# Strassen's product in four feed forward stages, its block products beside the down product

## The chip, the cores and the metric

The kernel runs on one core of one Trainium2 chip. The time is device microseconds of one execution. Two levels of TensorE's clock occur in such profiles, 1.2 and 2.4 GHz; the profile prints the granted one in tenths of full speed. The engines are TensorE (PE, with its weight loads as PEld), VectorE (DVE), ScalarE (ACT), GpSimd (POOL) and SyncE (SP, which only issues DMAs here).

## The reference

Two transformer blocks on 256 tokens of width 1024, all in float32. Eight stages follow one another: 0 feed forward, 1 attention and convolution, 2 feed forward, 3 feed forward, 4 gated linear attention, 5 feed forward (with these the first block is done), 6 the mixer of the second block, 7 its feed forward. All five feed forward stages compute the same kind of thing:

```python
def swiglu(x, w_in, w_out):
    a, b = jnp.split(x @ w_in, 2, axis=-1)
    return (jax.nn.silu(a) * b) @ w_out

# the first block, per layer
f = swiglu(rms_norm(h, g[0]), ffn1_w_in[l], ffn1_w_out[l])
h = h + FFN_RES * rms_norm(f, g[1])
# the second block
ffn = jnp.dot(jax.nn.silu(jnp.dot(h2, w_ffn_gate)) * jnp.dot(h2, w_ffn_up), w_ffn_down)
```

Here x is 256 x 1024, a and b have 2816 columns each, and w_out is 2816 x 1024. Besides, the second block needs `mod = silu(c) @ w_ada + b_ada` (1024 x 6144), which the kernel computes little by little beside the stages 0 to 5.

## The kernel before

**Exact products from split operands.** Each float32 operand is split in a high part (rounded to the type that TensorE multiplies fast) and the rest: `xh`, `xl` for the tokens, `whi`, `wlo` for the weights, `gh`, `gl` for the hidden values. A product is then three matmuls: high by high, high by rest, rest by high. Tokens are the stationary side (128 x 128), weights move (128 x 512), so one k block of 128 rows for one half of the tokens (`tok` 0 or 1) is three matmuls into one PSUM bank of 512 columns.

**Units and subunits.** `plan` is the list of weight units in the order of use: a unit is up to four k blocks of 512 columns (1 MB) and is loaded by SyncE into one of three `raw` buffers (`load_unit`, L480). Each unit gives subunits of two k blocks. For every subunit ScalarE writes `whi` (`split_hi`, L508) and VectorE `wlo` (`split_lo`, L524) into a ring of seven buffers (`NSPL`), and TensorE then spends 12 matmuls on it (6 for each half of the tokens). `whi` of subunit j waits for TensorE's last matmul on subunit j-7, and a unit's load waits for `wlo` of the unit three loads before it. ScalarE and VectorE walk the same list some five subunits ahead of TensorE (`ahead`, `LOOK`), and between the splits stand their other tasks, in the order in which the code is written: nothing is reordered at run time.

**A feed forward stage** has 11 chunks of 256 hidden columns. A chunk takes 256 columns of a and 256 of b (two units, four subunits, 48 matmuls), one bank for each half of the tokens. ScalarE then takes the silu (`act_silu`), VectorE multiplies (`dve_gate`) into `hid`, TensorE transposes the hidden values of two chunks at a time (`pe_hid_two`, L1143), ScalarE and VectorE split them (`act_ghi`, `dve_glo`). After the chunks comes the down product (`pe_down`, L854): 22 subunits of `w_out` (264 matmuls) into four banks, column half n = 0 or 1 by token half. At its end ScalarE squares the result, VectorE multiplies by a gain row and adds it to `h`, and the next stage opens.

**Strassen's product** is used in stage 7 alone (`STRASSEN = (7,)`). Chunks 8 and 9 together are x (256 x 1024) by a 1024 x 1024 block, which splits into four 512 x 512 blocks and two token halves by two k halves. Seven block products p1 to p7 of two subunits and 12 matmuls each (`pe_product`, L778) replace the eight of the plain way. Their moving sides are built by memory transfers that add: GpSimd issues them (`pool_strassen`, L561). p1's block is loaded into the tile `rows` (which elsewhere holds two gain rows), p5 adds a block to it, p3's block is loaded into `work`, p6 is the sum of both, made by VectorE (`dve_t2`, L543), then p4 adds a block to `rows` and p7 one to `work`. Each waits until the block before it in its tile has been split. p2 is a plain unit in the `raw` ring. The token sums are made by VectorE (`dve_sx`) and split like the rest into `sxh`, `sxl`. The seven results are combined in four banks a, b, c, d: ScalarE copies a at p1 (`act_part`, L819), and twice again, for VectorE's subtractions (`dve_combine`, L830), on which p3 and p4 wait. In stage 7 each product stands between two chunks (`sequence`): 0, 1, p1, 2, p2, 3, p5, 4, p6, 5, p3, 6, p7, 7, p4, 10.

**Beside it** SyncE's queue brings the 96 tiles of `w_ada` (256 KB each, `load_ada`, L637), one behind each of certain units; VectorE adds each into `adaacc` (L618), and twelve times folds a sum (`ada_sum`, L621). Each tile's load waits until VectorE has used the tile two before it, and SyncE issues nothing past that wait.

## Time and profile before

| | us |
|---|---|
| median of 3 runs | 1418.01 |
| lowest, highest | 1417.10, 1418.36 |
| the profiled execution, its own time | 1416.94 |
| its span in the profile | 1415.1 |
| TensorE busy | 1401.8 (99%) |
| VectorE busy | 956.5 (68%) |
| ScalarE busy | 731.7 (52%) |

Times in the profile run from the start of the span. Matmuls are pipelined, so that the time of one (389 ns in most rows) is longer than the distance from one to the next; a busy TensorE says that it is fed and not how fast it runs. An engine's idle time is put down to what released it. "Landing" is the time from a DMA's issue to its last byte.

### The profile page before, as it was taken

What the parts mean: (1) busy time and instruction counts of PE and PEld (TensorE: products, weight loads), DVE (VectorE), ACT (ScalarE), POOL (GpSimd) and SP (SyncE); (2) the same over time, 40 slices, a digit from 0 to 9 for tenths busy, and PEclk for the clock granted to TensorE, in tenths of its full rate; (3) what the DMA queues carried; (4) which work ended last, traced back from release to release, by engine and by line L of the source; (5) the groups of instructions that cost most, each with busy time, mean ns of one, the idle gap of its engine ahead of it and who ended that gap; (6) DMA issues with size and microseconds to landing.
All of it is one profiled execution on the core that took longest, in us unless ns stands there. A gap on an engine that the chain in (4) does not pass through costs nothing.

```text
span 1415.1 us, 19090 instructions
## 1 busy us (share of the span) xinstructions
PE 1401.8 (99%) x7327; PEld 1147.2 (81%) x7327; DVE 956.5 (68%) x1307; ACT 731.7 (52%) x1050; POOL 160.1 (11%) x242
## 2 busy tenths in 40 slices
PE   9999999999999999999999999999999999999997
PEld 7888888688888888888878888888877788888886
DVE  6666567886676667665787757755568566786654
ACT  6444455564443445543665545445655634655542
POOL 1600010000000000000172100000542110011000
PEclk9999999999999999999999999999999999999999
DMA  9585755256876778868544688764845355588551
GB/s 318 199 253 198 262 203 207 68 171 207 251 242 215 231 228 265 252 210 264 187 150 148 203 210 256 255 211 140 238 160 197 121 178 179 171 242 211 178 209 59
DMA packets 234857, 288.24 MB, mean 204 GB/s; under 512 B 37076, under 2 KB 156672, under 8 KB 234768
## 3 DMA queue, kind: packets, MB, share of 16 engines
q1 hardware_dynamic: 232160, 281.48, 61.6%
q0 software_dynamic: 2208, 5.24, 1.8%
q8 instruction: 58, 0.95, 0.3%
q10 hardware_dynamic: 400, 0.31, 0.1%
q14 instruction: 31, 0.25, 0.1%
HBM read 282.80 MB, written 4.20 MB: 203 GB/s over the span
## 4 chain that ended last, share of the span: by engine, by line
PE 95%; DVE 2%; issue 1%; ACT 1%; POOL 0%; POOLq 0%; ACTq 0%; DVEq 0%
PE ps L706 29%; PE ps L709 28%; PE ps L707 28%; PE pst L974 1%; PE pst L1155 1%; DVE wlo L532 1%; PE pst L1468 1%; PE ps L813 0%; PE ps L812 0%; PE ps L811 0%; PE ps L1415 0%; ACT whi L521 0%; PE ps L679 0%; PE pst L1782 0%; PE pst L2355 0%
## 5 line engine op out<-in xcount | busy, mean ns | idle before, releaser
L532 DVE TENSOR_TENSOR wlo<-raw,whi 128x1024 fp32r<-128x1024 f32 (+2 forms) x468 | 558.2, 1224 | 257.7 <-ACT whi L521 255.9
L521 ACT ACTIVATE whi<-raw 128x1024 fp32r<-128x1024 f32 (+2 forms) x468 | 467.8, 1040 | 244.2 <-PE ps L709 97.4
L706 PE MATMUL ps<-whi,xh 128*128 128x512 f32 (+4 forms) x1406 | 551.5, 392 | 1.6 <-ACT xh L1013 0.6
L707 PE MATMUL ps<-wlo,xh 128*128 128x512 f32 (+4 forms) x1406 | 541.1, 385 | 0.0
L709 PE MATMUL ps<-whi,xl 128*128 128x512 f32 (+4 forms) x1406 | 532.7, 385 | 0.0
L706 PEld LDWEIGHTS ps<-whi,xh 128*128 128x128 f32 x1406 | 263.9, 188 | 60.6 <-issue 4.7
L709 PEld LDWEIGHTS ps<-whi,xl 128*128 128x128 f32 x1406 | 263.9, 188 | 53.6
L707 PEld LDWEIGHTS ps<-wlo,xh 128*128 128x128 f32 x1406 | 264.2, 188 | 49.8
L706 PE MATMUL ps<-whi,gh 128*128 128x512 f32 x440 | 172.0, 391 | 0.0
L707 PE MATMUL ps<-wlo,gh 128*128 128x512 f32 x440 | 171.2, 389 | 0.0
L709 PE MATMUL ps<-whi,gl 128*128 128x512 f32 x440 | 153.4, 389 | 0.0
L1094 ACT ACTIVATE hid<-ps,st 128x256 f32<-128x256 f32 x88 | 41.3, 473 | 151.0 <-PE ps L709 151.0
L914 POOL TENSOR_SCALAR st<-st 128x1 f32<-128x1 f32 x26 | 10.5, 405 | 903.1 <-ACT work L900 903.1
L1100 DVE SCALAR_TENSOR_TENSOR hid<-ps,st,hid 128x256 f32<-128x256 f32 x88 | 41.8, 482 | 87.8 <-ACT hid L1094 87.7
L709 PEld LDWEIGHTS ps<-whi,gl 128*128 128x128 f32 x440 | 82.6, 188 | 17.3
L706 PEld LDWEIGHTS ps<-whi,gh 128*128 128x128 f32 x440 | 82.6, 188 | 16.9
L707 PEld LDWEIGHTS ps<-wlo,gh 128*128 128x128 f32 x440 | 82.6, 188 | 16.8
L618 DVE SCALAR_TENSOR_TENSOR adaacc<-adat,scol,adaacc 128x512 f32<-128x512 f32 x84 | 62.7, 746 | 0.0
L1170 ACT ACTIVATE gh<-pst 128x1024 fp32r<-128x1024 f32 x25 | 25.5, 1020 | 20.9 <-PE pst L1155 20.7
L1179 DVE TENSOR_TENSOR gl<-pst,gh 128x1024 fp32r<-128x1024 f32 x25 | 30.5, 1221 | 8.1 <-ACT gh L1170 8.1
L900 ACT ACTIVATE work<-h 128x512 f32<-128x512 f32 x36 | 22.4, 627 | 20.3 <-DVE h L2249 18.9
L1613 DVE SCALAR_TENSOR_TENSOR Y<-cx,vcol,Y 128x256 f32<-128x256 f32 x79 | 32.4, 480 | 0.0
(306 smaller groups left out, 956.0 us busy)
## 6 DMA issues: line engine op xcount, KB each, us to landing
raw<-in_ffn_w_in_dram SPq DMA_DIRECT2D x174, 512.0 KB, 5.3
raw<-in_ffn_w_out_dram SPq DMA_DIRECT2D x40, 1024.0 KB, 5.5
raw<-in_w_in_dram SPq DMA_DIRECT2D x26, 1024.0 KB, 4.8
adat<-in_w_ada_dram SPq DMA_DIRECT2D x96, 256.0 KB, 2.8
raw<-in_hyb_w_in_dram SPq DMA_DIRECT2D x10, 1024.0 KB, 5.1
raw<-in_gla_w_in_dram SPq DMA_DIRECT2D x10, 1024.0 KB, 5.2
raw<-in_w_ffn_down_dram SPq DMA_DIRECT2D x10, 1024.0 KB, 5.0
raw<-in_w_ffn_gate_dram SPq DMA_DIRECT2D x18, 512.0 KB, 3.9
```

The costliest lines, as they stand in the source:

```text
L521: e.activation(split_of(whi, j), raw_of(j), ACT.Copy).then_inc(*whi_made.up(j))
L532: e.tensor_tensor(split_of(wlo, j), raw_of(j), split_of(whi, j).bitcast(F32), ALU.subtract).then_inc(*wlo_made.up(j))
L618: e.scalar_tensor_tensor(adaacc[:, :], adat[n % 2][:, :], sc, adaacc[:, :], ALU.mult, ALU.add).then_inc(*ada_added.up(c, k))
L706: e.matmul(ps[:, 0:n], a, whi_of(j, k), start=first and k == 0, stop=False)
L707: last = e.matmul(ps[:, 0:n], a, wlo_of(j, k), start=False, stop=False)
L709: last = e.matmul(ps[:, 0:n], b, whi_of(j, k), start=False, stop=final and k == subs[j][2] - 1)
L900: e.activation(spare[:, 0:src.shape[1]], src, ACT.Square, scale=scale, accum_out=col(2, "ss", key)[:, i:i + 1]).then_inc(*squares.up(key, i))
L1094: e.activation(hb[:, tok * 512 + 256:tok * 512 + 512], acc.of(st, JC[st, c], tok)[:, 0:256], ACT.Silu, scale=rstd(("h", st, tok)) if st < ...
L1100: e.scalar_tensor_tensor(hb[:, tok * 512:tok * 512 + 256], acc.of(st, JC[st, c], tok)[:, 256:512], rstd(("h", st, tok)) if st < 7 else 1.0 ...
L1170: e.activation(halves_of(gh[:, c * 512:(c + 2) * 512]), turned_halves, ACT.Copy).then_inc(*ghi_made.up(st, c))
L1179: e.tensor_tensor(halves_of(gl[:, x]), turned_halves, halves_of(gh[:, x]).bitcast(F32), ALU.subtract).then_inc(*glo_made.up(st, c))
L1613: e.scalar_tensor_tensor(y_of(b), cx_of(b, k), conv_w(b, k), y_of(b), ALU.mult, ALU.add).then_inc(*tap_made.up(b, k))
```

## The change

Stages 2, 3, 5 and 7 now take chunks 8 and 9 by Strassen's product. Their order is new, in stage 7 too: chunks 0 to 7, p1, chunk 10, and then the down product, in whose first columns the other six products stand. The down product of these stages goes through 16 k blocks for column half 0, through the same for half 1, and then through the last six for both (before: four k blocks for half 0, the same for half 1, and so on). With i the number of the down subunit, p5 stands ahead of i = 2, p6 ahead of 4, p3 and p2 ahead of 6, p7 ahead of 10, p4 ahead of 12 (`BESIDE`). The banks of column half 1 are the ones that b and d leave. The hidden values of chunks 8 and 9 are transposed at i = 14 and used from i = 16 on.

The token sums are spread over chunks 3 to 5. The tiles of `w_ada` skip the units that have no load on SyncE's queue, so they stand a little closer. The gain rows of these stages are loaded in the middle of the down product, since `rows` holds weight blocks until then. Two small transfers that write gate values to memory (4 KB, element by element) are now eight pieces each.

```diff
@@ -279,16 +279,18 @@
                         plan.append(([(w[k * P:(k + m) * P, n * 512:(n + 1) * 512]
                                        .rearrange("(k p) n -> p k n", p=P), 0, 512)], m, 512))
 
-        STRASSEN = (7,)
+        STRASSEN = (2, 3, 5, 7)
         PAIR = 8
         BLOCK = {"p1": ("x1", 0, 0), "p2": ("ring", 1, 0), "p5": ("x1", 0, 1), "p6": ("x1", None, None),
                  "p3": ("x2", 1, 1), "p7": ("x2", 0, 1), "p4": ("x1", 1, 0)}
-        product_unit, home, chunk_unit, down_unit = {}, {}, {}, {}
+        BESIDE = {2: ("p5",), 4: ("p6",), 6: ("p3", "p2"), 10: ("p7",), 12: ("p4",)}
+        mixed_units = [(k, min(4, k1 - k), n) for k0, k1 in ((0, 16), (16, 22)) for n in range(2) for k in range(k0, k1, 4)]
+        product_unit, home, chunk_unit, down_unit, down_units = {}, {}, {}, {}, {}
 
         def sequence(st):
 
             if st in STRASSEN:
-                return (0, 1, "p1", 2, "p2", 3, "p5", 4, "p6", 5, "p3", 6, "p7", 7, "p4", 10)
+                return (*range(8), "p1", 10)
             return tuple(range(11))
 
...
@@ -314,7 +316,15 @@
                 else:
                     plan_parts([(w, c * 256, 256) for w in w_in], 8)
             down_unit[st] = len(plan)
-            plan_down(w_out, 22)
+            if st not in STRASSEN:
+                plan_down(w_out, 22)
+                return
+            for i, (k, m, n) in enumerate(mixed_units):
+                for name in BESIDE.get(2 * i, ()):
+                    plan_product(st, w_in, name)
+                down_units.setdefault(st, []).append(len(plan))
+                plan.append(([(w_out[k * P:(k + m) * P, n * 512:(n + 1) * 512]
+                               .rearrange("(k p) n -> p k n", p=P), 0, 512)], m, 512))
 
 
         GLA_COLS = (((512, 512),), ((256, 256), (3072, 16)), ((0, 256),), ((1024, 512),), ((1536, 512),), ((2048, 512),),
...
@@ -400,14 +411,15 @@
 
 
         ada_view = T["w_ada_2"].rearrange("(p k) n -> p k n", k=8)
-        ada_units = [u for st in (0, 2, 3, 5) for u in range(U0[st] + (8 if st == 0 else 0), U0[st + 1])]
+        ada_units = [u for st in (0, 2, 3, 5) for u in range(U0[st] + (8 if st == 0 else 0), U0[st + 1]) if u not in home]
...
@@ -538,7 +550,7 @@
                     if u in ada_summed:
                         ada_sum(e, ada_summed[u])
 
...
@@ -564,10 +576,10 @@
                 e.wait_ge(*wlo_made.at(last_sub[product_unit[st, name]]))
             e.wait_ge(*f_scaled.at(st - 1, 1, 1))
             pool_product(e, st, "p1", False)
+            e.wait_ge(*xlo_made.at(st, "sums", 1))
+            pool_product(e, st, "p3", False)
             split("p1")
             pool_product(e, st, "p5", True)
-            e.wait_ge(*xlo_made.at(st, "sums"))
-            pool_product(e, st, "p3", False)
             split("p6")
             pool_product(e, st, "p4", True)
             split("p3")
...
@@ -778,19 +798,19 @@
         def pe_product(e, st, name, base):
 
             bank, tile, first, until = {
-                "p1": ("a", 4, True, (silu_made, st, PAIR, 1)), "p2": ("b", None, False, None),
-                "p5": ("c", 5, True, (gated, st, PAIR, 1)), "p3": ("d", 3, False, (gated, st, PAIR, 0)),
+                "p1": ("a", 0, True, (silu_made, st, PAIR, 1)), "p2": ("b", None, False, None),
...
             if name == "p1":
-                acc.next((st, "b"), (silu_made, st, PAIR, 0), tile=base + 2)
+                acc.next((st, "b"), (silu_made, st, PAIR, 0), tile=base + 3)
                 b_freed[st] = acc.freed
             ps = acc.of(st, bank)
             if name == "p5":
-                e.wait_ge(*xlo_made.at(st, "sums"))
+                e.wait_ge(*xlo_made.at(st, "sums", 1))
             if name == "p2":
                 e.wait_ge(*part_made.at(st, "p1"))
...
@@ -830,6 +850,8 @@
         def dve_combine(e, st, name):
 
             e.wait_ge(*part_made.at(st, name))
+            if name == "p6":
+                e.wait_ge(*gated.at(st, 10, 1))
             d = acc.of(st, "d" if name == "p6" else "c")
             e.tensor_tensor(d[:, :], acc.of(st, "c")[:, :], part[:, :], ALU.subtract
...
+        def down_sub(j0, i):
+            return DSUB[j0][i] if j0 in DSUB else j0 + i
+
+        def mixed_order():
+            return [(q, n) for k, m, n in mixed_units for q in range(k, k + m, 2)]
...
@@ -857,21 +885,28 @@
 
 
             bank, freed = {}, {}
-            for tok in range(2):
-                for n in range(2):
-                    bank[tok, n] = acc.next((key, tok, n), *readers(tok, n))
-                    freed[tok, n] = acc.freed
-            order = down_order(nk)
+
+            def take(tok, n, tile=None):
+                bank[tok, n] = acc.next((key, tok, n), *readers(tok, n), tile=tile)
+                freed[tok, n] = acc.freed
+            mixed = j0 in DSUB
+            if not mixed:
+                for tok in range(2):
+                    for n in range(2):
+                        take(tok, n)
+            order = mixed_order() if mixed else down_order(nk)
 
             def one(i, tok):
                 q, n = order[i]
                 if q == 0:
+                    if mixed:
+                        take(tok, n, acc.n + 2 + 2 * tok + n)
                     for done in freed[tok, n]:
                         e.wait_ge(*done)
...
@@ -1187,20 +1226,16 @@
                 enter(e, st, 0)
                 pe_warm(e, 4)
             pe_first(e, st, j0, lambda: enter(e, st, 1), readers)
-            base = acc.n - 4
             for c in sequence(st)[2:]:
                 if c in BLOCK:
-                    pe_product(e, st, c, base)
-                    if c == "p4":
-                        pe_hid_two(e, st, PAIR - 2)
+                    pe_product(e, st, c, acc.n)
                     continue
 
                 def at(i, c=c):
-                    if c % 2 == 0 and i == (3 if st in STRASSEN and c == 10 else 2):
-                        pe_hid_two(e, st, c - 2)
-                pe_chunk(e, st, JC[st, c], readers[c], at, (base, base + 1) if st in STRASSEN else (None, None))
-            if st in STRASSEN:
-                acc.n += 4
+                    if c % 2 == 0 and i == 2:
+                        pe_hid_two(e, st, before(st, c))
+                mixed = c == 10 and st in STRASSEN
+                pe_chunk(e, st, JC[st, c], readers[c], at, (acc.n + 1, acc.n + 5) if mixed else (None, None))
 
         def entry(e, st):
 
...
@@ -1213,6 +1248,11 @@
             j1 = JD[st]
 
             def at(i):
+                if st in STRASSEN:
+                    for name in BESIDE.get(i, ()):
+                        pe_product(e, st, name, acc.n)
+                    if i == 14:
+                        pe_hid_two(e, st, PAIR)
                 if i == 2:
...
@@ -1222,37 +1262,44 @@
                     lambda q, tok: (ghi_made.at(st, turn_of(q // 2)), glo_made.at(st, turn_of(q // 2))), readers, at, lag=LAG[st],
                     then=entry(e, st + 1))
 
...
-                    if st in STRASSEN and (c, i) == (2, 1):
-                        act_sx(e, st)
+                    if mixed and (c, i) == (10, 2):
+                        act_part(e, st, "p1")
+                    if mixed and (c, i) in SX_HI:
+                        act_sx(e, st, SX_HI.index((c, i)))
                 if c % 2 == 0:
-                    act_ghi(e, st, c - 2)
+                    act_ghi(e, st, before(st, c))
                 act_silu(e, st, c, 0)
                 act_silu(e, st, c, 1)
             for i in range(22):
-                act_begin(e, JD[st] + i)
+                for name in BESIDE.get(i, ()) if mixed else ():
+                    for half in range(2):
+                        act_begin(e, JP[st, name] + half)
+                act_begin(e, down_sub(JD[st], i))
                 if i == 2:
                     act_ghi(e, st, 10)
+                if mixed and i in (5, 11):
+                    act_part(e, st, "p6" if i == 5 else "p7")
+                if mixed and i in (7, 13):
+                    act_silu_pair(e, st, i // 13)
+                if mixed and i == 15:
+                    act_ghi(e, st, PAIR)
 
         def dve_ffn(e, st):
             j0 = J0[st]
...
@@ -2952,14 +3003,19 @@
             pool_diags(e)
             pool_open(e, 1)
             pool_open(e, 2)
+            pool_strassen(e, 2)
             pool_open(e, 3)
+            pool_strassen(e, 3)
             pool_gla(e)
             pool_open(e, 5)
+            pool_strassen(e, 5)
             pool_m2(e)
             pool_ada_open(e, 7)
             pool_strassen(e, 7)
             for tok in range(2):
                 pool_pow(e, ("h", 8, tok))
+
+        gate_piece = {u0 + b: (which, b) for which, u0 in ((2, U0[5] + 10), (5, U0[6] + 8)) for b in range(8)}
 
         def sp_program(e):
             for i, n in enumerate((0, 512)):
@@ -2984,17 +3040,19 @@
                         e.dma_start(wg[:, :], T["gla_w_gate"][0]).then_inc(*s_wg.up())
                     if st == 6:
                         load_row(e, "gn", T["gn_w_2"], D, [gla_normed.at(1, 3)])
-                if u in (U0[5] + 10, U0[6] + 8):
-                    i, which = (0, 2) if u < U0[6] else (1, 5)
-                    e.wait_ge(*mod_made.at(2 * which + 1))
-                    e.dma_start(gate_rows[i].rearrange("(b p) -> p b", p=P), modc[:, which * 8:which * 8 + 8],
-                                allow_slow_non_contiguous=True).then_inc(*s_gates.up(which))
-                if u == U0[6] + 10:
+                if u in gate_piece:
+                    which, b = gate_piece[u]
+                    if b == 0:
+                        e.wait_ge(*mod_made.at(2 * which + 1))
+                    e.dma_start(gate_rows[which // 5][b * P:(b + 1) * P].rearrange("(p o) -> p o", o=1),
+                                modc[:, which * 8 + b:which * 8 + b + 1], allow_slow_non_contiguous=True
+                                ).then_inc(*s_gates.up(which))
+                if u == U0[6] + 16:
                     load_row(e, "g2", gate_rows[0], D, [s_gates.at(2), f_scaled.at(5, 1, 1)])
-                if u == (down_unit[7] if 7 in STRASSEN else U0[7] + 4):
+                if u == (down_units[7][8] if 7 in STRASSEN else U0[7] + 4):
                     load_row(e, "g5", gate_rows[1], D, [s_gates.at(5), gr_made.at(1, 1), *rows_free(7)])
                 for st in STRASSEN:
-                    if u == down_unit[st] and st in gains:
+                    if u == down_units[st][8] and st in gains:
                         load_row(e, st, gains[st], D, rows_free(st))
                 if u == U0[4] + 7:
                     o = const_at["lev"][0]
```

Two places in the program's order, all in stage 2 (the others are alike). In the rows `whi` and `wlo` are the parts of a subunit of weights, and what they are made from tells what it is: `raw` a plain unit, `rows` p1, p5, p6 or p4, `work` p3 or p7.

VectorE before, from the gates of chunk 10 (L1100) into the down product:

```order
L1100 SCALAR_TENSOR_TENSOR hid<-ps,st,hid 128x256 x2
L532 TENSOR_TENSOR wlo<-raw,whi 128x1024 x3
L1175 TENSOR_TENSOR gl<-pst,gh 128x512
L532 TENSOR_TENSOR wlo<-raw,whi 128x1024
L615 TENSOR_SCALAR adaacc<-adat,scol 128x512
L532 TENSOR_TENSOR wlo<-raw,whi 128x1024 x2
L618 SCALAR_TENSOR_TENSOR adaacc<-adat,scol,adaacc 128x512
```

The same place now:

```order
L1136 SCALAR_TENSOR_TENSOR hid<-ps,st,hid 128x256 x2
L560 TENSOR_TENSOR rows<-rows,work 128x2048
L544 TENSOR_TENSOR wlo<-raw,whi 128x1024 x2
L544 TENSOR_TENSOR wlo<-rows,whi 128x1024 x2
L638 SCALAR_TENSOR_TENSOR adaacc<-adat,scol,adaacc 128x512
L544 TENSOR_TENSOR wlo<-raw,whi 128x1024
L1214 TENSOR_TENSOR gl<-pst,gh 128x512
L544 TENSOR_TENSOR wlo<-raw,whi 128x1024
L544 TENSOR_TENSOR wlo<-work,whi 128x1024 x2
L544 TENSOR_TENSOR wlo<-raw,whi 128x1024 x2
L856 TENSOR_TENSOR ps<-ps,part 128x512
```

Between the last gate of chunk 10 and the subtraction (L856) that p3 waits for stand the sum of p6 (L560), ten splits and two smaller operations.

ScalarE now, from the splits of p3 (`work`, the second row) to the silu of token half 0 of chunks 8 and 9 (L1153), which leaves bank b:

```order
L533 ACTIVATE whi<-raw 128x1024
L533 ACTIVATE whi<-work 128x1024 x2
L533 ACTIVATE whi<-raw 128x1024 x2
L847 ACTIVATE part<-ps 128x512
L533 ACTIVATE whi<-raw 128x1024 x4
L533 ACTIVATE whi<-work 128x1024 x2
L1153 ACTIVATE hid<-ps,st 128x2x256
```

ScalarE before, from chunk 10 on, had splits of plain units and nothing else in the down product (the last row):

```order
L521 ACTIVATE whi<-raw 128x1024 x4
L1170 ACTIVATE gh<-pst 128x2x8x64
L1094 ACTIVATE hid<-ps,st 128x256 x2
L521 ACTIVATE whi<-raw 128x1024 x3
L1168 ACTIVATE gh<-pst 128x512
L521 ACTIVATE whi<-raw 128x1024 x17
```

The copy (L847) and the silu now stand among the splits, and the silu stands behind the two splits of p7.

GpSimd, whose queue had nothing but the small operations of the norms in stages 2, 3 and 5, now issues ten half-unit transfers in each of them, ahead of the norms of the next stage: two for p1, two for p3, then two each that add, for p5, p4 and p7.

## Rows read from the trace of the kernel before

**Rows 1.** The page: engines, TensorE's clock over 40 slices, the chain by engine.
```profile
PE 1401.8 (99%) x7327; PEld 1147.2 (81%) x7327; DVE 956.5 (68%) x1307; ACT 731.7 (52%) x1050; POOL 160.1 (11%) x242
...
PEclk9999999999999999999999999999999999999999
...
PE 95%; DVE 2%; issue 1%; ACT 1%; POOL 0%; POOLq 0%; ACTq 0%; DVEq 0%
```

**Rows 2.** Chain of waits in order of time: start us, us, what.
```profile
336.81 0.64 PE pst L1155 x16
...
427.36 0.64 PE pst L1155 x16
...
821.22 0.64 PE pst L1155 x16
...
911.77 0.64 PE pst L1155 x16
...
1256.16 0.65 PE pst L1155 x16
...
1343.99 0.65 PE pst L1155 x16
```

**Rows 3.** Timeline of TensorE: start us, us, line, operation; first and last of 27.
```profile
299.63 0.39 PE L706 MATMUL ps<-whi,xh 128*128 128x512 f32 x1
...
305.53 0.39 PE L709 MATMUL ps<-whi,xl 128*128 128x512 f32 x1
```

**Rows 4.** Instruction groups, shapes apart, whole span: busy us, mean ns.
```profile
L618 DVE SCALAR_TENSOR_TENSOR adaacc<-adat,scol,adaacc 128x512 f32<-128x512 f32 x84 | 62.7, 746 | 0.0
...
L811 PE MATMUL ps<-whi,sxh 128*128 128x512 f32 x16 | 6.2, 389 | 0.0
```

**Rows 5.** The same for VectorE, window 1240 to 1350 (stage 7).
```profile
L532 DVE TENSOR_TENSOR wlo<-raw,whi 128x1024 fp32r<-128x1024 f32 x35 | 41.3, 1220 | 5.4 <-ACT whi L521 5.4
...
L548 DVE TENSOR_TENSOR rows<-rows,work 128x2048 f32<-128x2048 f32 x1 | 2.3, 2291 | 0.0
L605 DVE TENSOR_TENSOR sxl<-work,sxh 128x2048 fp32r<-128x2048 f32 x1 | 2.3, 2282 | 0.0
L834 DVE TENSOR_TENSOR ps<-ps,part 128x512 f32<-128x512 f32 x2 | 1.4, 693 | 0.0
...
L589 DVE TENSOR_TENSOR work<-xh,xl 128x1024 f32<-128x1024 f32 x1 | 1.2, 1215 | 0.0
```

**Rows 6.** The same for ScalarE, same window.
```profile
L521 ACT ACTIVATE whi<-raw 128x1024 fp32r<-128x1024 f32 x37 | 37.3, 1053 | 4.3 <-DMA raw<-in_w_ffn_up_dram 3.5 <-PE ps L709 0.8
...
L827 ACT ACTIVATE part<-ps 128x512 f32<-128x512 f32 x2 | 1.2, 580 | 0.0
```

**Rows 7.** Timeline of GpSimd's DMA issues, stage 7.
```profile
1266.36 1.50 POOL L559 DMA_DIRECT2D work<-in_w_ffn_up_dram  x2 [18.58 <-DVE sxl L605]
1282.43 2.48 POOL L557 DMA_DIRECT2D rows<-in_w_ffn_gate_dram  x2 [14.57 <-DVE wlo L532]
1296.89 2.42 POOL L557 DMA_DIRECT2D work<-in_w_ffn_up_dram  x2 [11.98 <-DVE wlo L532]
```

**Rows 8.** Timeline of ScalarE beside them.
```profile
1309.15 1.06 ACT L521 ACTIVATE whi<-work 128x1024 fp32r<-128x1024 f32 x1 [1.73 <-DMA work<-in_w_ffn_up_dram]
```

**Rows 9.** DMA queues, window 1278 to 1311: packets, MB, share of 16 engines.
```profile
q1 hardware_dynamic: 5371, 5.33, 52.0%
q0 software_dynamic: 1088, 2.10, 38.6%
```

**Rows 10.** Windows: length, busy us by engine, clock, DMA share, GB/s.
```profile
872.00:883.00 11.00, 11.00 (x50) 9.13 (x49) 6.95 (x9) 4.86 (x6) 0.00 (x0) 1.00 0.81 229
1289.00:1300.00 11.00, 11.00 (x50) 9.09 (x49) 8.36 (x9) 6.95 (x9) 2.42 (x2) 1.00 0.89 220
```

**Rows 11.** DMA issues, whole span: KB each, median us to landing.
```profile
raw<-in_ffn_w_out_dram SPq DMA_DIRECT2D x40, 1024.0 KB, 5.5
...
gate_rows<-modc SPq DMA_DIRECT2D x2, 4.0 KB, 12.4
```

More of the change, by code:

```diff
@@ L360, in program @@
         JD = {st: first_sub[u] for st, u in down_unit.items()}
+        DSUB = {JD[st]: [j for u in us for j in range(first_sub[u], last_sub[u] + 1)] for st, us in down_units.items()}
         JC = {key: first_sub[u] for key, u in chunk_unit.items()}
@@ new lines, in act_sx, with dve_sx_lo @@
+        def act_sx(e, st, half):
+            o = slice(half * 1024, (half + 1) * 1024)
+            e.wait_ge(*summed.at(st, "x", "p3"))
+            e.activation(sxh[:, o], workx[:, o], ACT.Copy).then_inc(*xhi_made.up(st, "sums", half))
+        def dve_sx_lo(e, st, half):
+            o = slice(half * 1024, (half + 1) * 1024)
+            e.wait_ge(*xhi_made.at(st, "sums", half))
+            e.tensor_tensor(sxl[:, o], workx[:, o], sxh[:, o].bitcast(F32), ALU.subtract
+                            ).then_inc(*xlo_made.up(st, "sums", half))
@@ L888, in down_last @@
         def down_last(j0, nk, n):
-            return j0 + max(i for i, (q, m) in enumerate(down_order(nk)) if m == n)
+            order = mixed_order() if j0 in DSUB else down_order(nk)
+            return down_sub(j0, max(i for i, (q, m) in enumerate(order) if m == n))
         halves = Ring([junk[:, 0:512], junk[:, 512:1024]])
@@ L1126, in dve_gate_pair, with before @@
                                    ).then_inc(*gated.up(st, PAIR, tok))
+        def before(st, c):
+            return 6 if c == 10 and st in STRASSEN else c - 2
         def turn_of(c):
@@ L1223, in pe_ffn, with act_ffn @@
                     then=entry(e, st + 1))
-        COMBINE = {2: "p1", 5: "p6", 7: "p7"}
-        def act_ffn(e, st, before):
+        SX_AT = [(3, 0), (3, 1), (3, 2), (3, 3), (4, 0)]
+        SX_HI, SX_LO = [(5, 0), (5, 2)], [(5, 1), (5, 3)]
+        def act_ffn(e, st, opening):
             j0 = J0[st]
@@ L1231, in act_ffn @@
             else:
-                act_open(e, st, before, lambda tok: act_silu(e, st, 0, tok))
+                act_open(e, st, opening, lambda tok: act_silu(e, st, 0, tok))
+            mixed = st in STRASSEN
             for c in sequence(st)[1:]:
@@ L1273, in dve_ffn @@
                     dve_begin(e, JC[st, c] + i)
[L1274 to L1275 removed]
+                    if mixed and (c, i) in SX_AT:
+                        dve_sx(e, st, SX_AT.index((c, i)))
+                    if mixed and (c, i) in SX_LO:
+                        dve_sx_lo(e, st, SX_LO.index((c, i)))
                 if c % 2 == 0:
[L1277 removed]
+                    dve_glo(e, st, before(st, c))
                 dve_gate(e, st, c, 0)
                 dve_gate(e, st, c, 1)
[L1280 to L1283 removed]
             for i in range(22):
[L1285 removed]
+                for name in BESIDE.get(i, ()) if mixed else ():
+                    for half in range(2):
+                        dve_begin(e, JP[st, name] + half)
+                dve_begin(e, down_sub(JD[st], i))
                 if i == 2:
                     dve_glo(e, st, 10)
+                if mixed and i in (5, 11):
+                    dve_combine(e, st, "p6" if i == 5 else "p7")
+                if mixed and i in (7, 13):
+                    dve_gate_pair(e, st, i // 13)
+                if mixed and i == 15:
+                    dve_glo(e, st, PAIR)
         hyb_gate = sig("hyb_gate")
```

79 lines of the change are left out of this document (32 added, 47 removed).

## The prediction

> **What bounds the kernel now.** The page comes first: TensorE is busy for 1401.8 of 1415.1 us, its clock shows full speed in all 40 slices (that is 2.4 GHz), and the chain that ends last is 95% TensorE [rows 1]. So time goes only where TensorE has fewer matmuls, or stands still less; VectorE at 68% and ScalarE at 52% have room on the average, and what is to be asked of them is whether they are late at one place.
>
> Next, what a matmul costs. From the first to the last of 27 matmuls in a row it takes 305.53 - 299.63 = 5.90 us for 26 distances, 0.227 us each [rows 3]; the 0.39 us printed for one is its length in the pipeline. A subunit or a block product (12 matmuls) is 2.72 us.
>
> Then, what Strassen's product has brought where it is already used. The chain shows the transposes of hidden chunks 0 and of chunks 8: between them lie 8 chunks, 384 matmuls, in the plain stages, and they take 427.36 - 336.81 = 90.55 us in stage 2 and 911.77 - 821.22 = 90.55 in stage 5. In stage 7, p1 lies ahead of the first and one subunit more ahead of the last, so there are 372, and they take 1343.99 - 1256.16 = 87.83 us [rows 2]. The difference is 2.72 us for 12 matmuls, just their own time: the block products of stage 7 cost TensorE no wait. A matmul on the token sums takes the same 389 ns as the others [rows 4].
>
> **The change part by part.**
>
> *Removed.* In each of stages 2, 3 and 5, eight blocks of 12 matmuls become seven. 3 x 12 x 0.2267 us = 8.16 us off TensorE. Stage 7 had seven already: nothing. Transposes are as many as before.
>
> *Added on VectorE*, per new stage, by the rows of stage 7 [rows 5]: 1.2 (sum of the parts of x), 4 x 0.7 (token sums, of the size of a combination), 2.3 (their rest, now in two halves), 2.3 (p6's sum), 2 x 0.69 (combinations), less two splits of 1.22 each since there are 14 subunits and not 16. That is 10.0 - 2.4 = 7.6 us in a stage of some 187 us, in which a plain stage leaves VectorE a third of its time. *On ScalarE*: 1.9 for the sums and 3 x 0.58 for copies, less 2 x 1.05 [rows 6]: 1.5 us. Both lie beside TensorE. On the average they cost nothing; so the places where TensorE waits for one of them are worked through.
>
> *p3 waits for the combination of c and p6's copy.* Behind p6 TensorE has two down subunits, 5.44 us. VectorE must have done, from the last gate of chunk 10 on: 2.3 + 10 x 1.22 + 0.75 + 0.7 = 16.0 us of other work, by the order shown ahead of L856 [rows 4, 5]. It starts some 1.4 us behind chunk 10's last matmul (a silu and a gate), so it is through at 17.4. TensorE reaches p6's end after two down subunits, p5, two more and p6: 4 x 2.72 + 2 x 2.72 = 16.3 us. Copy (0.58) and subtraction (0.69) then end near 18.7, and p3 starts at 21.8. There are 3 us to spare. For the first subunit behind p6's sum it is 1.4 + 2.3 + 1.22 = 4.9 against 8.2. p4's wait for the second combination has two subunits of cover as well, and less work ahead of it. The transposes of chunks 8 and 9 come 5.44 us behind p4, for a silu and a gate of 0.7 each.
>
> *p7's weights, and what is queued behind them.* This is the tightest place. ScalarE's silu of the pair stands behind the splits of p7, so if p7's block lands late, bank b stays taken, and the first down subunit of column half 1 (i = 8) waits; the gate that leaves bank d waits with it. The adding transfer of p7 goes out when p3's second subunit has been split. Its `whi` may be written once the first down subunit behind p5 is done, so the issue comes when TensorE is near the end of the second, just ahead of p6. From there to the half of i = 8 in which bank d is needed: p6, two down subunits, p3 and p2, two down subunits, half a subunit, 2.72 x 7.5 = 20.3 us. Behind the landing stand a split on each engine, the silu and the gate (taken like the subtraction of as many columns): 1.05 + 1.22 + 0.7 + 0.7 [rows 5, 6], so the landing must come within some 16.6 us of the issue. In stage 7 the same transfer was issued at 1296.89, and ScalarE, which had waited 1.73 us for it, began on its second half at 1309.15: 12.3 us [rows 7, 8]. But there p4's transfer had gone 14.5 us ahead of it (1282.43) and was done. Now p4's goes 8.2 us ahead (p5 and two subunits), and queues in front. Two such pairs took 38.6% of 33 us of all engines, 6.4 us each, while the other queue took 52.0% [rows 9]. If p4 is not out of the way, p7 is 2 to 4 us later: 14 to 16 us. That is still inside 16.6, with little to spare in stage 5, where all eight tiles of a `w_ada` column come beside it. So I put the wait at 0, with 0 as its lower bound and up to 2 us a stage (8 us) as its upper one.
>
> *Load on the memory engines.* In the 33 us of rows 9 both queues had 91%. With a tile of 0.25 MB to each of five units, that queue's 5.33 MB become 6.6, its 52% 64%, and the sum 103%. The backlog is 1 us over this stretch. Five or six subunits of lead on ScalarE and VectorE hide it; a plain unit lands 5.5 us after its issue [rows 11] and, with products between the units, is wanted 8 to 11 us after it. VectorE in such a window of stage 7 was busy for 8.36 of 11 us, in a plain one of stage 5 for 6.95, at 0.89 and 0.81 of the memory engines [rows 10].
>
> *The rest.* The gain rows are issued behind p4's split, ten down subunits or 27 us ahead of their use, five times a plain unit's landing [rows 11]. The writes of gate values (12.4 us landing for 4 KB) [rows 11] come in pieces, and nothing waits for them soon. Tiles of `w_ada` a little closer together add no work. GpSimd was idle in these stages until their last norms. I take 0 for all of these, and plus or minus 0.5 us for them together.
>
> *Sum.* 1416.94 - 8.16 = 1408.8 for the profiled execution. It lies 1.07 under the median, so the median becomes 1418.01 - 8.16 = 1409.9. I forecast 1410.0 us.
>
> **The rivals.**
>
> *Late blocks (still faster).* p7's or p5's block is 1 to 2 us past its limit in the stages with `w_ada` tiles, perhaps in all four. For it: the 103% above, and the 8.2 us between p4 and p7 in place of 14.5. Against it: the lead that all splits have, and waits of ScalarE for blocks in stage 7 of only 1.7 us. It gives 1410 + 3 x 1.3, about 1414.
>
> *Two adding transfers in a line (slower).* When both queues are full, p7 starts only when p4 is done, and both run at half rate. If each then takes 12.3 us, p4 ends 12.3 - 8.2 = 4.1 us after p7's issue, and a p7 that is served as slowly again as it was (twice 12.3 us less the 2.5 of issuing, 22 us) lands at 26. TensorE would stand still 26 - 16.6 = 9 us at i = 8 in each of four stages: 1410 + 37 = 1447. It turns the change to a loss from 8.16 / 4 = 2.0 us of standing a stage on, which is a landing of 18.6 us.
>
> *GpSimd's issue is held by VectorE (slower).* The pair of adding transfers costs GpSimd 2.4 us and a pair of plain ones 1.5 [rows 7]. If it could write only while VectorE stands still, which is 24% of the time in that window [rows 10], a pair would take 2.48 / 0.24 = 10.3 us and land 7.8 us later: 20.1 against 16.6, so 3.5 us a stage and 1410 + 14 = 1424. Stage 7's own rows speak against it: 2.4 us with VectorE 76% busy. The Trainium skill, page "SBUF — State Buffer", section "SBUF: two separate sides", has a rule of this kind: while VectorE runs an operation in a two-port mode, GpSimd is locked out and cannot write the descriptors of its own DMAs. By that rule this case would be the one that comes; nothing in this trace shows a wait of that length.
>
> *No change that can be told.* Stands of 1.4 to 2.7 us in each of the four stages (the limit passed by a little everywhere) would eat 5.4 to 11 us: 1418. That the change does not do what it says I exclude: the order of TensorE has 36 matmuls fewer.
>
> **How the numbers follow.** A measurement of this kernel tells a change from 0.2% on (2.8 us; its three runs lie within 1.3 us). My forecast 0.74, late blocks 0.13, no change 0.07, two transfers in a line 0.03, GpSimd held 0.03. Faster takes the first two: 0.87. Same 0.07. Slower 0.06. The first case by itself is 1408.9 to 1411; the range goes up over late blocks, to 1415, and down to 1408.5 for the 0.5 us of the small terms and the spread of the runs.
>
> **What would show it.** Right: 7291 matmuls on the page and not 7327; 90.55 us become less by one block product in stages 2, 3 and 5; idle time of TensorE ahead of the block products and of the down subunits i = 8 stays at a few tenths; the sum of TensorE's busy time is near 1393.6. Wrong: TensorE waiting for VectorE at L856 or for the silu of the pair at i = 8, ScalarE waiting over 5 us for `work` or `rows` blocks, DMA landings on GpSimd's queue over 17 us. The time is off if these stands come in several stages, or if a stage's opening is later because the gain row or the last folds of `w_ada` are.

## The result, and the profile after

| | median us | lowest, highest | runs |
|---|---|---|---|
| before | 1417.17 | 1416.88, 1418.36 | 6 |
| changed | 1432.66 | 1429.01, 1437.18 | 6 |

The ratio is 1.0109, with a 95% interval of 1.0092 to 1.0127: 15.5 us slower. The forecast was 1410.0 us, 8.2 us faster; it missed by 22.7 us and had the wrong sign.

The page of the changed kernel, the lines that answer to [rows 1]:

```profile
PE 1398.4 (98%) x7291; PEld 1142.7 (80%) x7291; DVE 1001.0 (70%) x1350; ACT 759.5 (53%) x1078; POOL 192.5 (13%) x272
...
PEclk9999999999999999999999998999999999999999
...
PE 84%; DMA 5%; DVE 5%; ACT 2%; issue 2%; SPq 1%; POOL 0%; POOLq 0%; ACTq 0%; DVEq 0%
```

The 36 matmuls are gone (7327 to 7291), but the chain that ends last is TensorE for 84% of the span and not for 95%; memory transfers, VectorE's splits and SyncE's issues now stand in it. One slice shows a lower clock.

Where does it stand still? Who TensorE waited for (total, times, longest us):

```profile
PE pst L1194 <- DVE hid L1136: 8.6, 2, 8.3
PE ps L726 <- DVE wlo L544: 6.6, 2, 6.1
```

Both long waits, 8.25 and 6.08 us, lie in stage 5. The other new stages did what was forecast. The chain's first transposes of the opening of stage 3 and of stage 4, before and then after:

```profile
492.63 0.87 PE pst L974 x8
...
678.85 0.88 PE pst L974 x8
```

```profile
489.62 0.87 PE pst L1010 x8
...
673.17 0.87 PE pst L1010 x8
```

186.22 us became 183.55: 2.67 us less, with 2.72 expected. In stage 2 the same distance went from 186.7 to 184.4. The loss is in stage 5: from its first transposes to stage 6's first matmul it took 194.6 us before (790.5 to 985.1) and takes 215.1 now (785.2 to 1000.3), where 191.9 was expected. Four windows of it (length, busy us by engine, clock, DMA share, GB/s):

```profile
856.00:867.00 11.00, 6.74 (x30) 5.26 (x28) 3.43 (x4) 2.95 (x4) 0.00 (x0) 1.00 1.02 168
867.00:878.00 11.00, 7.01 (x37) 5.77 (x38) 6.83 (x8) 2.73 (x5) 1.44 (x2) 0.69 0.76 91
878.00:889.00 11.00, 6.49 (x29) 5.05 (x27) 0.00 (x0) 0.80 (x1) 0.00 (x0) 0.97 1.06 257
889.00:900.00 11.00, 9.43 (x32) 7.62 (x33) 10.71 (x13) 8.57 (x13) 2.50 (x2) 0.71 0.93 242
```

TensorE is fed for some 60% of the first three. The granted clock falls to 0.69 and 0.71 of 2.4 GHz in two windows around the stands, so part of them ran at 1.2 GHz. TensorE's five stands in the stage add up to 18.3 us (1.48, 8.25, 6.08, 0.92, 1.58); the stage lost 23.2. The lower clock accounts for the 5 us between: by the clock column (0.69, 0.97 and 0.71 of 11 us each) it could take at most 3.4 + 0.3 + 3.2 = 6.9 us, an estimate, and less where TensorE stood anyway.

How a load came to be late is seen in the chain of waits, first on the way to the stands (start us, us, what):

```profile
833.13 0.35 SPq L663
833.48 0.04 issue
833.52 0.43 SPq L3047
833.95 0.04 issue
834.00 0.43 SPq L506
834.43 0.04 issue
834.47 11.83 DMA raw<-in_ffn_w_in_dram
846.30 0.02 issue
846.32 1.07 ACT whi L533
```

L663 is a tile of `w_ada`, L3047 a piece of the gate values (128 values of 4 bytes), L506 a weight load. The weight load (two halves of 512 KB each; the median landing of such a load in this kernel is 5.7 us) takes 11.83 us behind the piece. The load behind the third piece takes as long (852.25 to 864.03). Its splits come late, and VectorE has two of them, an addition into `adaacc` and the rest of a token sum (L624, 1.22 us) ahead of the gates that end the first long stand at 870.99. The load behind the fifth piece takes 17.89 us and ends the second stand, at 890.57:

```profile
868.95 0.34 SPq L663
...
869.33 0.43 SPq L3047
...
869.81 0.43 SPq L506
...
870.29 17.89 DMA raw<-in_ffn_w_in_dram
...
888.20 1.06 ACT whi L533
...
889.29 1.24 DVE wlo L544
...
890.57 0.79 PE ps L726
```

ScalarE's waits for these loads:

```profile
846.32 2.01 ACT L533 ACTIVATE whi<-raw 128x1024 fp32r<-128x1024 f32 x2 [9.26 <-DMA raw<-in_ffn_w_in_dram]
...
864.05 1.06 ACT L533 ACTIVATE whi<-raw 128x1024 fp32r<-128x1024 f32 x1 [8.90 <-DMA raw<-in_ffn_w_in_dram]
...
888.20 2.00 ACT L533 ACTIVATE whi<-raw 128x1024 fp32r<-128x1024 f32 x2 [13.91 <-DMA raw<-in_ffn_w_in_dram]
```

Before, the two longest such waits in this stage were these:

```profile
848.43 2.01 ACT L521 ACTIVATE whi<-raw 128x1024 fp32r<-128x1024 f32 x2 [6.95 <-DMA raw<-in_ffn_w_in_dram]
...
858.73 2.01 ACT L521 ACTIVATE whi<-raw 128x1024 fp32r<-128x1024 f32 x2 [4.54 <-DMA raw<-in_ffn_w_in_dram]
```

While a piece is under way little is moved, though the memory engines count as busy for about half of the time. DMA share and GB/s of the window 833.6 to 846.4 in 40 slices of 0.32 us, and the landing of two pieces:

```profile
DMA  0566847939962439216982675412869998999999
GB/s 0 83 115 256 302 104 128 74 29 35 35 26 64 128 109 86 26 38 48 54 29 26 45 26 54 58 42 90 182 189 320 368 368 326 374 372 391 385 365 323
...
gate_rows<-modc SPq DMA_DIRECT2D x2, 0.5 KB, 9.1
```

From slice 8 to slice 26 (some 6 us, counted from 0) 26 to 128 GB/s are moved, and some 320 to 390 behind it. The rate comes back near 842.2; the pieces issued at 833.52 and 840.18 have a median landing of 9.1 us. So the trace puts the slow stretch beside the piece; whether the piece is its cause is asked by e1 and e2.

### The profile page after: what moved, and what is told of

Same layout as the page of the kernel before. It is cut to its first block, busy times and chain, and to the rows that moved or that the text cites. A ratio compares the mean times of both kernels' runs of the same rounds, so it can differ in the third digit from the quotient of the medians.

```text
span 1430.1 us, 19155 instructions
## 1 busy us (share of the span) xinstructions
PE 1398.4 (98%) x7291; PEld 1142.7 (80%) x7291; DVE 1001.0 (70%) x1350; ACT 759.5 (53%) x1078; POOL 192.5 (13%) x272
## 4 chain that ended last, share of the span: by engine, by line
PE 84%; DMA 5%; DVE 5%; ACT 2%; issue 2%; SPq 1%; POOL 0%; POOLq 0%; ACTq 0%; DVEq 0%
PE ps L726 24%; PE ps L729 24%; PE ps L727 24%; DMA raw<-in_ffn_w_in_dram 4%; DVE wlo L544 3%; PE ps L833 2%; PE ps L832 2%; PE ps L831 2%; PE pst L1010 1%; ACT whi L533 1%; PE pst L1194 1%; DMA raw<-in_ffn_w_out_dram 1%; PE pst L1519 1%; DMA raw<-in_gla_w_in_dram 0%; DVE adaacc L638 0%
## 5 line engine op out<-in xcount | busy, mean ns | idle before, releaser
L544 DVE TENSOR_TENSOR wlo<-raw,whi 128x1024 fp32r<-128x1024 f32 (+2 forms) x450 | 539.5, 1224 | 274.4 <-ACT whi L533 270.9
L533 ACT ACTIVATE whi<-raw 128x1024 fp32r<-128x1024 f32 (+2 forms) x450 | 452.0, 1040 | 285.6 <-DMA raw<-in_ffn_w_in_dram 114.7
L726 PE MATMUL ps<-whi,xh 128*128 128x512 f32 (+2 forms) x1310 | 515.5, 394 | 9.1 <-DVE wlo L544 6.6
L727 PE MATMUL ps<-wlo,xh 128*128 128x512 f32 (+2 forms) x1310 | 505.2, 386 | 0.0
L729 PE MATMUL ps<-whi,xl 128*128 128x512 f32 (+2 forms) x1310 | 496.6, 386 | 0.0
L726 PEld LDWEIGHTS ps<-whi,xh 128*128 128x128 f32 x1310 | 246.9, 188 | 65.0 <-DVE wlo L544 8.9
L729 PEld LDWEIGHTS ps<-whi,xl 128*128 128x128 f32 x1310 | 246.8, 188 | 50.2
L727 PEld LDWEIGHTS ps<-wlo,xh 128*128 128x128 f32 x1310 | 247.1, 189 | 46.4
L726 PEld LDWEIGHTS ps<-whi,gh 128*128 128x128 f32 x440 | 82.6, 188 | 20.4 <-DVE hid L1160 2.0
L544 DVE TENSOR_TENSOR wlo<-rows,whi 128x1024 fp32r<-128x1024 f32 x32 | 38.0, 1220 | 7.1 <-ACT whi L533 7.0
L533 ACT ACTIVATE whi<-rows 128x1024 fp32r<-128x1024 f32 x32 | 32.9, 1055 | 15.9 <-PE ps L729 10.0
L936 ACT ACTIVATE work<-h 128x512 f32<-128x512 f32 x36 | 22.4, 626 | 20.3 <-DVE h L2300 18.9
```

What stands on the lines that cost most here:

```text
L533: e.activation(split_of(whi, j), raw_of(j), ACT.Copy).then_inc(*whi_made.up(j))
L544: e.tensor_tensor(split_of(wlo, j), raw_of(j), split_of(whi, j).bitcast(F32), ALU.subtract).then_inc(*wlo_made.up(j))
L726: e.matmul(ps[:, 0:n], a, whi_of(j, k), start=first and k == 0, stop=False)
L727: last = e.matmul(ps[:, 0:n], a, wlo_of(j, k), start=False, stop=False)
L729: last = e.matmul(ps[:, 0:n], b, whi_of(j, k), start=False, stop=final and k == subs[j][2] - 1)
```

## Experiments

The theory after this look, called G: the pieces of the gate write are the cause. Against it stood A (GpSimd's adding transfers beside `w_ada` tiles) and W (the tiles of `w_ada` standing closer).

**e1.** The gate values in one transfer again.

```diff
-                if u in gate_piece: ... gate_rows[which // 5][b * P:(b + 1) * P] <- modc[:, which * 8 + b]
+                if u in (U0[5] + 10, U0[6] + 8):
+                    e.dma_start(gate_rows[i].rearrange("(b p) -> p b", p=P), modc[:, which * 8:which * 8 + 8], ...)
```

> The changed kernel, with the gate values written in one transfer again (at the units where the first piece stands). Theory G (each of the eight pieces holds up the weight load that is queued behind it on SyncE's queue, some 6 us each, and in stage 5 the load has no slack because each w_ada tile's wait keeps it back): the loss of stage 5 goes, 1409 to 1411 us. Rival A (the adding transfers of GpSimd's queue beside w_ada tiles are what makes the loads of stage 5 land after 12 to 18 us): stays near 1430. Rival W (the w_ada tiles standing closer): stays near 1430.

1420.62 us (1416.72 to 1423.89, 10 runs), ratio 1.0025 [1.0015, 1.0034]. The pieces are worth 12.0 us, but 10.7 us to the worked-out 1409.9 are left: G is half of it. (The kept trace is of the fastest of the ten, 1416.72, so it shows little of what is left.)

**e2.** The kernel before with the pieces alone.

```diff
+                if u in gate_piece: (as in the change)
```

> The kernel before, with the gate values written in eight pieces and nothing else changed. Theory G: slower than before by 10 to 20 us, all of it in stage 5. Rivals A and W: 1417, no change.

1430.10 us, ratio 1.0094 [1.0076, 1.0111]: 13.0 us with no block product in stage 5. ScalarE's waits for weight loads in stage 5 (total, times, longest) before and in e2:

```profile
ACT whi L521 <- DMA raw<-in_ffn_w_in_dram: 23.8, 10, 6.9
```

```profile
ACT whi L521 <- DMA raw<-in_ffn_w_in_dram: 59.3, 12, 9.6
```

**e3.** The kernel before with the new spacing of `w_ada` alone.

```diff
+            i = min(10 * c, c * 106 // 11)
-                ada_tiles[ada_units[10 * c + k]] = c, k     (sent +11, read +12, summed +13)
+                ada_tiles[ada_units[i + k]] = c, k          (sent +10, read +11, summed +12)
```

> The kernel before, with the w_ada tiles spaced as in the changed kernel (a new column every 9 or 10 units, sums one unit earlier). Theory G and rival A: 1417, within 1 us. Rival W: slower by several us.

1422.47 us, ratio 1.0037 [1.0024, 1.0050]: 5.4 us slower, where G and A had no change. W is true as well. Its stand is elsewhere, at stage 2's first chunks (2.87 us, and the clock at 0.84 behind it). What moved there is SyncE's queue. e3, then before:

```profile
321.93 0.34 SPq L644 DMA_DIRECT2D adat<-in_w_ada_dram  x1
322.37 1.81 SPq L656 DMA_DIRECT2D fold<-ada_out  x4
324.22 0.43 SPq L504 DMA_DIRECT2D rows<-in_norm_g_dram  x1
324.70 0.99 SPq L495 DMA_DIRECT2D raw<-in_ffn_w_in_dram  x2
```

```profile
321.92 0.92 SPq L494 DMA_DIRECT2D raw<-in_ffn_w_in_dram  x2
330.14 0.34 SPq L643 DMA_DIRECT2D adat<-in_w_ada_dram  x1
330.58 1.80 SPq L655 DMA_DIRECT2D fold<-ada_out  x4
```

The weight load that went out at 321.92 now goes out at 324.70, behind a tile that waited for VectorE, four reads of a folded sum (1.81 us of issuing) and a gain row. It lands at 333.04, and ScalarE and VectorE come too late. VectorE then has the fold of a sum ahead of the gate that TensorE waits for (337.10 to 338.62), which is part of the 2.87 us. A second stand, 0.97 us at the opening of stage 3, has an addition into `adaacc` ahead of the norm.

This run is not the edit as it stands in the change. In the changed kernel the gain row is no longer in this place of the queue: the weight load goes out at 323.63, lands at 329.85, and TensorE has no stand there over 0.32 us. So the 5.4 us are the price of the spacing in the kernel before, and no run has the block products with the old spacing.

**e4.** The changed kernel with stage 5 plain.

```diff
-        STRASSEN = (2, 3, 5, 7)
+        STRASSEN = (2, 3, 7)
...
-            pool_strassen(e, 5)
```

> The changed kernel with stage 5 left plain (Strassen in 2, 3 and 7), the eight pieces kept. Theory G: the loss of stage 5 stays for the most part, 1424 to 1432 us. Rival A: the loss goes with the adding transfers of stage 5, 1412 us (two stages' gain of 2.7 us each).

1438.05 us, ratio 1.0147 [1.0132, 1.0162]. The loss is larger and not smaller: the loss doesn't need the block products of stage 5, and A as its cause falls. Why the loss is larger was not shown: six of the seven products bring no load on SyncE's queue, which may give it more time between two loads; but the edit also moves the tiles, since the list of units that can carry one grows from 119 to 122.

What G and W share became theory Q: a tile's load waits until VectorE has used the tile two before it, and what is queued behind it, the next weight load, waits with it. So in the stages with `w_ada` a weight load goes out shortly ahead of its need, whatever the three `raw` buffers allow: the one issued at 332.42 in the kernel before was wanted by ScalarE 1.4 us later (it waited from 333.79 to 338.01). Anything that makes it later or slower then reaches TensorE.

**e5.** e1 with a third buffer for the tiles.

```diff
-        s_ada = [sig(f"s_ada{i}", 16) for i in range(2)]
+        s_ada = [sig(f"s_ada{i}", 16) for i in range(3)]
...
+                adat.append(sb("adat2", 512, where=tail))
-                part = sb("part", 512, where=tail)
+                part = hidx[:, 512:1024]
...
-                    e.wait_ge(*ada_added.at(*divmod(n - 2, 8)))
+                    e.wait_ge(*ada_added.at(*divmod(n - 3, 8)))
```

> The changed kernel with one gate write, and with three buffers for the tiles of w_ada in place of two, so that SyncE's queue waits for VectorE's use of the tile three before and not two before. (p6's and p7's copy goes to a half of hid that is free then, to make room.) Theory Q (what is left of the loss comes from weight loads held back behind the waits for w_ada tiles on SyncE's queue): the waits at the openings of stage 5 and at its chunks go, 1411 to 1413 us; the two waits at i = 8 of stage 5's down product (2.5 us together) stay. Rival A (memory engines are full): no better than 1420.

1409.81 us (1409.25 to 1410.02), ratio 0.9947 [0.9933, 0.9962]. That is 10.8 us from e1, and 7.1 us faster than the kernel before (1416.88 beside it). It is better than Q had it (1411 to 1413): the two waits at i = 8, which Q kept, are gone as well. ScalarE's waits for loads of `w_in` in stage 5 are down from 48.9 us in the changed kernel (30.6 in the trace of e1) to 5.5:

```profile
ACT whi L533 <- DMA raw<-in_ffn_w_in_dram: 48.9, 9, 13.9
```

```profile
ACT whi L534 <- DMA raw<-in_ffn_w_in_dram: 5.5, 2, 5.1
```

**e6.** e5 with p7's transfer issued ahead of p4's.

```diff
+            split("p3")
+            pool_product(e, st, "p7", True)
             split("p6")
             pool_product(e, st, "p4", True)
-            split("p3")
-            pool_product(e, st, "p7", True)
```

> As e5, and GpSimd issues p7's adding transfer ahead of p4's. Theory P (p7's block lands late because p4's stands ahead of it in the same queue): the two waits at i = 8 of stage 5 go too, 1409 to 1410 us. Rival (p7 is late because its own issue is): the two waits stay, as e5.

1410.26 us, ratio 0.9950 [0.9933, 0.9967]: the same as e5. The two waits at i = 8 were gone in e5 already, so that neither case was tested; e5 had left p7's transfer where it was, so they had not come from its place in the queue. In the changed kernel ScalarE's splits of p7 (`work`) started right behind one of a plain unit that had waited 7.54 us for its load:

```profile
942.48 2.01 ACT L533 ACTIVATE whi<-raw 128x1024 fp32r<-128x1024 f32 x2 [7.54 <-DMA raw<-in_ffn_w_out_dram]
944.39 1.99 ACT L533 ACTIVATE whi<-work 128x1024 fp32r<-128x1024 f32 x2
```

**e7.** The third buffer in the kernel before, nothing else.

```diff
...
-                    e.wait_ge(*ada_added.at(*divmod(n - 2, 8)))
+                    e.wait_ge(*ada_added.at(*divmod(n - 3, 8)))
```

> The kernel before with the third buffer for w_ada tiles alone (it shares its place with the tile part, which only stage 7 uses). Theory Q: 1417, no change, since TensorE did not wait in before. A gain would mean that the third buffer is worth something by itself.

1416.72 us, ratio 0.9999 [0.9989, 1.0008]: no change, as expected. The buffer is slack that the kernel before does not need.

**e8.** e2 with the third buffer (the same edit).

> The kernel before with the eight gate pieces and the third buffer. Theory Q: each piece makes the load behind it some 6 us longer, but loads go out earlier, so much of the 13 us of e2 goes: 1418 to 1424 us. If the piece's cost doesn't depend on the slack of the loads: 1430 as e2.

1419.99 us (1418.64 to 1426.15), ratio 1.0026 [1.0015, 1.0036]. Of 13.0 us that the pieces cost, 10 go.

**e9.** The changed kernel with the third buffer, pieces kept.

> The changed kernel with its eight gate pieces kept and the third buffer for w_ada tiles. Theory Q (loads with no slack are what turns a slow transfer into a wait of TensorE) gives 1411 to 1416 us: as e8 stands to before, 3 us above e5. If pieces and adding transfers make each other worse: 1420 or more.

1424.33 us (1418.17 to 1426.87, 10 runs), ratio 1.0041 [1.0027, 1.0056]. The buffer alone brings 8.3 us, but it is 14.5 us above e5 and not 3. This is the second case of the expectation (1420 or more): in the changed kernel the pieces cost more than in the kernel before, and the third buffer doesn't cover it. Whether that comes from the adding transfers, the new order or the spacing is open, and so is how the runs come to spread over 8.7 us; the kept trace is of the fastest one, 1418.17.

**e10.** The changed kernel with `STRASSEN = (7,)`, one gate write, old spacing of `w_ada`: the new places alone.

> The changed kernel with Strassen's product in stage 7 alone, one gate write, and w_ada tiles spaced as before: what is left is the new places of the six products in stage 7's down product. All theories: 1417, no change; a loss here would be a price of the new places themselves.

1417.43 us, ratio 0.9999 [0.9989, 1.0008]: the new places cost nothing in stage 7.

**e11.** The kernel before with the whole gate write eight times in stage 5.

```diff
-                if u in (U0[5] + 10, U0[6] + 8):
+                if u in [U0[5] + 10 + b for b in range(8)] + [U0[6] + 8]:
```

> The kernel before with the whole gate write (4 KB, 1024 values of 4 bytes) made eight times in stage 5, at the eight places of e2's pieces, to eight different rows. If a transfer costs by its number of values, eight times the values of e2: some 60 us or more above before. If it costs mostly by itself, whatever its size: like e2, 1425 to 1435 us.

1457.12 us, ratio 1.0277 [1.0255, 1.0299]: 39.7 us, between the two cases. Eight times the values of e2 cost three times its 13.0 us.

**e12.** The changed kernel, stage 5's pieces issued by ScalarE.

```diff
+                if u in gate_piece and j == first_sub[u]:   (in split_hi, ahead of the unit's first split)
+                    e.dma_start(gate_rows[...], modc[...]).then_inc(*s_gates.up(which))
```

> The changed kernel (two buffers for w_ada tiles), the eight pieces of stage 5 issued by ScalarE's queue and not SyncE's; stage 6's write is one transfer. If the weight loads are held by standing behind the piece in their own queue: near 1420 us, as e1. If the piece holds up the memory engines for every queue: near 1430 us, as the changed kernel.

1440.35 us, ratio 1.0152 [1.0131, 1.0173]. A piece on another queue holds the weight loads up as well; it is 7.7 us worse than on SyncE's queue, which neither case had, and why was not looked into. ScalarE issues a piece at 849.75, SyncE the load at 850.80:

```profile
850.80 0.98 SPq L506 DMA_DIRECT2D raw<-in_ffn_w_in_dram  x2
```

```profile
849.75 0.33 ACTq L531 DMA_DIRECT2D gate_rows<-modc  x1
859.33 1.06 ACT L542 ACTIVATE whi<-raw 128x1024 fp32r<-128x1024 f32 x1 [9.11 <-DMA raw<-in_ffn_w_in_dram]
```

## Why the prediction was wrong

**Right.** The price of a matmul and the sum for the block products: 2.67 us off stage 3 with 2.72 forecast, and TensorE busy for 1393.1 us in e5 where 1393.6 was given (1398.4 in the changed kernel). With one gate write and the third buffer the whole kernel stands at 1409.8 (e5). That it meets the worked-out 1409.9 is in part luck: against the 1416.88 measured beside it, it is 7.1 us faster and not 8.2, and a stand of 1.5 us that the change brought (below) is still in it. VectorE's extra work and p3's wait cost nothing where no load was late: no wait for the subtraction at L856 is among TensorE's, and e10 shows the new places free in stage 7. (In the changed kernel the rest of a token sum does stand between the late load and the end of the 8.25 us.) That GpSimd's issue might be held by VectorE did not happen: 2.43 us for a pair in stage 5 of e5 at 901.60 and 909.07.

```profile
901.60 2.43 POOL L570 DMA_DIRECT2D rows<-in_ffn_w_in_dram  x2 [26.77 <-DVE wlo L545]
909.07 2.43 POOL L570 DMA_DIRECT2D work<-in_ffn_w_in_dram  x2 [5.04 <-DVE wlo L545]
```

The rule that the prediction set beside that case is one for operations in a two-port mode. No row here shows VectorE's operations in such a mode, so it was not shown that by this rule the case would have to come.

**The step that failed** is the paragraph "The rest", which took 0 for two edits. "The writes of gate values come in pieces, and nothing waits for them soon": the pieces were priced by who waits for them. The price is what is queued behind them, 13.0 us by themselves (e2). With them back in one transfer the changed kernel is 12.0 us faster (e1). "Tiles of `w_ada` a little closer together add no work": they add none, but they move other things, in two queues. On SyncE's queue they move the issue of a weight load; the new spacing by itself cost 5.4 us in the kernel before (e3). On VectorE they put the fold of a sum at the opening of stage 5, ahead of the norm's first operation (L1034, L998 before), for which ScalarE and then TensorE wait. Before, and then after:

```profile
790.69 0.75 DVE L618 SCALAR_TENSOR_TENSOR adaacc<-adat,scol,adaacc 128x512 f32<-128x512 f32 x1
791.35 1.28 DVE L998 TENSOR_TENSOR work<-pst,vcol 128x512 f32<-128x512 f32 x2
```

```profile
786.05 0.42 DVE L645 TENSOR_TENSOR fold<-fold 128x256 f32<-128x256 f32 x1
...
787.58 1.29 DVE L1034 TENSOR_TENSOR work<-pst,vcol 128x512 f32<-128x512 f32 x2
```

That operation starts 0.88 us behind the stage's first transposes (790.47) before and 2.40 us behind them (785.18) now; the 1.52 us between are the fold, and TensorE's stand of 1.48 us there is its price. The prediction named "the last folds of `w_ada`" among the signs of being wrong, and still took 0.

The prices measured one by one, -8.2 for the block products, 13.0 for the pieces (e2) and 5.4 for the spacing (e3), make 1427.4 of the 1432.7. This is a sum of prices from other kernels and not a division of the loss: e3's stand in stage 2 is not in the changed kernel, and e4 and e9 show that the parts do not just add. What is shown of the changed kernel is 12.0 us for the pieces, and 10.8 more that a third tile buffer takes away. How much of these 10.8 comes from the spacing and how much from the new order and the adding transfers stays open.

**A second error made the first look safe.** The text had a plain unit "wanted 8 to 11 us" behind its issue and named no row for it. In the changed kernel the loads issued at 834.00, 851.77 and 869.81 were wanted by ScalarE (the start of its wait) at 837.06, 855.15 and 874.29, 3.1 to 4.5 us later, less than the 5.5 us of a landing. The front part said that SyncE issues nothing past a tile's wait, and the trace had shown ScalarE waiting up to 6.95 us for loads in stage 5: where `w_ada` runs, the slack was near zero. e5, e7 and e8 bear it out: the same third buffer is worth 10.8 and 10.1 us where something is late, and nothing where nothing is. (In the working on p7, 7.5 x 2.72 is 20.4 us and not 20.3; nothing hangs on it.)

**The rivals.** The cases of late blocks and of two adding transfers in a line rested on p7. In e5 p7's second half was split at 921.59, having waited 1.93 us, 12.5 us behind the first issue at 909.07; the same 12.3 us as in stage 7 before [rows 7, 8], and not 14 to 16, though p4's transfer went out only 7.5 us ahead:

```profile
921.59 1.06 ACT L534 ACTIVATE whi<-work 128x1024 fp32r<-128x1024 f32 x1 [1.93 <-DMA work<-in_ffn_w_in_dram]
```

The wait at i = 8 that they foresaw did occur in the changed kernel (0.92 and 1.58 us), but behind a plain load that was late (e6). The case for the slower side had its mechanism in the wrong queue, and its chance of 0.06 left out what SyncE's queue holds.

**Open.** The old spacing of `w_ada` with all the block products was not run, nor a gate write placed where no tile is beside it, nor the changed kernel with the fold moved away from stage 5's opening.

## What to carry to other kernels

Price each edit on an in-order queue by what stands behind it: a transfer that nobody waits for, or a tile moved by one place, can hold the next load up. Ask first how much slack that load has, from the wait that really lets it go and not from the number of its buffers; one more buffer on the side stream that shares the queue (e5) can be worth more than the tuned change itself. Where small work of a side stream is moved, look at what each engine's own order then puts ahead of a stage's opening. Cutting a slow scattered write in eight is no cure for its time.

## What the runs showed of the hardware

- A write of 128 values of 4 bytes from 128 partitions to memory landed after 9.8 to 14.1 us (medians of e12 and of e8 and e9; 12.5 in the changed kernel), about as long as the 12.4 us of 1024 values in one transfer [rows 11]. Beside it all queues together moved 26 to 128 GB/s for about 6 us, while the memory engines counted as half busy. Issued from ScalarE's queue it held the weight loads up as well (e12).
- Eight such small writes cost 13.0 us, eight of eight times the values 39.7 us, where the loads behind them had no slack.
- In stage 5 of the changed kernel, with stands of 18.3 us TensorE lost 23.2 us, with a granted clock of 0.69 and 0.71 in two windows beside them.
- With two adding transfers issued 7.5 us apart, the second was in use 12.5 us after its issue (e5); with two issued 14.5 us apart, 12.3 us after it [rows 7, 8].
